# Sample attention of a hybrid decoder layer: the suffix bias added by a small matmul, and cache pages loaded in 32 pieces of 8 KB

## What is computed

```python
kp = cache_k[page_table].reshape(DB, past, H, Dh)      # 8 sequences x 16 pages x 128 tokens
vp = cache_v[page_table].reshape(DB, past, H, Dh)
lfp = cache_logf[page_table].reshape(DB, past, H).astype(jnp.float32)
suffix = (lax.cumsum(lfp, axis=1, reverse=True) - lfp).transpose(0, 2, 1)
cn = jnp.cumsum(logf, axis=1).transpose(0, 2, 1)
s_past = jnp.einsum('bqhd,bkhd->bhqk', q, kp).astype(jnp.float32) * scale
s_past = s_past + suffix[:, :, None, :] + cn[:, :, :, None]
...
p = jax.nn.softmax(jnp.concatenate([s_past, s_new], axis=-1), axis=-1)
o = (jnp.einsum('bhqk,bkhd->bqhd', p[..., :past].astype(v.dtype), vp)
     + jnp.einsum('bhqk,bkhd->bqhd', p[..., past:].astype(v.dtype), v))
```

## Time and profile before

| | before |
|---|---|
| median of 3 runs | 2228.1 us |
| the profiled execution, its own time | 2225.12 us |
| its span, first to last instruction | 2223.5 us |
| sample attention in it | from about 846 to 1119 us |
| mean granted TensorE clock | 0.941 |
| TensorE busy (matmuls) | 1988.0 us, 89% |
| VectorE, ScalarE, GpSimd busy | 591.6, 303.0, 190.3 us |
| DMA | 401.00 MB in 100543 packets, mean 180 GB/s |

### The profile page before, as it was taken

One profiled execution on the slowest core, in us unless ns is written; L12 is line 12 of the kernel. 1 busy time (PEld: TensorE's weight loads), 2 busy tenths in 40 slices (PEclk: granted clock), 3 DMA queues, 4 the chain that ended last, 5 costly groups with the idle time before them and its releaser, 6 DMA issues. The chain is left out here.

```text
span 2223.5 us, 22907 instructions
## 1 busy us (share of the span) xinstructions
PE 1988.0 (89%) x8429; PEld 1087.9 (49%) x8429; DVE 591.6 (27%) x1287; ACT 303.0 (14%) x489; POOL 190.3 (9%) x280
## 2 busy tenths in 40 slices
PE   8999989799999992877689999479999999994997
PEld 4474445466666662545455555334444444441443
DVE  4201124222222222434223222611111111101776
ACT  1000001122222220323211000000000000000111
POOL 1000013000000001123300000000000000001221
PEclk9989999899999995989789999679999999996999
DMA  6020100701020007999742123279999999993220
GB/s 241 14 78 1 41 20 1 290 30 68 30 72 30 31 24 231 263 317 301 244 167 80 48 76 146 85 285 402 419 418 424 425 419 420 422 370 105 69 79 28
DMA packets 100543, 401.00 MB, mean 180 GB/s; under 512 B 18809, under 2 KB 28090, under 8 KB 87634
## 3 DMA queue, kind: packets, MB, share of 16 engines
q1 hardware_dynamic: 76866, 326.02, 38.4%
q0 software_dynamic: 16496, 56.15, 7.5%
q10 hardware_dynamic: 7072, 17.38, 2.0%
HBM read 353.69 MB, written 45.81 MB: 180 GB/s over the span
## 5 line engine op out<-in xcount | busy, mean ns | idle before, releaser
L1791 PE MATMUL psum<-arena 128*64 128x512 f32 (+1 forms) x1024 | 343.8, 598 | 1.4 <-DVE arena L1881 1.4
L774 PE MATMUL psum<-arena 128*128 128x363 f32 (+1 forms) x768 | 256.7, 477 | 13.9 <-DMA arena<-in_w_in 11.2
L1791 PEld LDWEIGHTS psum<-arena 128*64 128x64 f32 (+1 forms) x1024 | 130.0, 165 | 180.9 <-issue 179.1
L287 PE MATMUL psum<-arena 128*128 128x512 f32 x432 | 189.6, 599 | 0.3 <-DMA arena<-in_w_in 0.3
L774 PEld LDWEIGHTS psum<-arena 128*128 128x128 f32 x768 | 139.7, 192 | 84.6 <-DMA arena<-in_w_in 11.3
L1828 PE MATMUL psum<-arena 128*64 128x512 f32 (+1 forms) x512 | 170.0, 595 | 1.0 <-DVE arena L1895 1.0
L975 PE MATMUL psum<-ident,arena 128*128 128x128 f32 x512 | 80.0, 306 | 66.4 <-DMA arena<-in_cache_k 50.1
L287 PEld LDWEIGHTS psum<-arena 128*128 128x128 f32 x432 | 82.3, 193 | 100.7 <-issue 99.9
L1387 PE MATMUL psum<-arena 128*128 128x512 f32 x288 | 125.7, 594 | 1.6 <-PEq L1244 1.6
L2154 PE MATMUL psum<-arena 128*128 128x512 f32 x288 | 125.1, 592 | 0.0
L1828 PEld LDWEIGHTS psum<-arena 128*64 128x64 f32 (+1 forms) x512 | 66.1, 163 | 101.9 <-issue 101.9
(11 more groups left out here) (262 smaller groups left out, 1943.8 us busy)
## 6 DMA issues: line engine op xcount, KB each, us to landing
arena<-in_w_exp_gate SPq DMA_DIRECT2D x32, 2048.0 KB, 13.6
arena<-in_w_exp_up SPq DMA_DIRECT2D x32, 2048.0 KB, 14.1
arena<-in_w_exp_down SPq DMA_DIRECT2D x32, 2048.0 KB, 10.7
arena<-in_cache_v POOLq DMA_DIRECT2D x128, 256.0 KB, 6.6
arena<-in_cache_k SPq DMA_DIRECT2D x128, 256.0 KB, 9.5
arena<-in_w_in SPq DMA_DIRECT2D x9, 2048.0 KB, 10.8
moe_out<-arena ACTq DMA_DIRECT2D x24, 512.0 KB, 11.8
moe_out<-arena SPq DMA_DIRECT2D x1, 9728.0 KB, 38.0
```

Source lines behind the costliest of these rows:

```text
L287: last = mm(c.bank[4 + r % 3][:, :], HT[:, k, t * P:(t + 1) * P], W[:, n + 1, k, :], start=(k == 0), stop=(k == KD - 1))
L774: last = mm(c.bank[7][:, 0:b - a], WG[:, blk % 2, k, q * P:(q + 1) * P], HT[:, k, a:b], start=(k == 0), stop=(k == KD - 1))
L1791: last = mm(out[rows_, :], XT[:, u % 2, k, rows_], c.ring_tile(LOAD[kind, u, r])[:, k, :], start=(k == 0), stop=(k == KD - 1))
```

## The change

The bias is no longer copied to each row by DMA. One load for each sequence brings the 8 heads' rows into 8 partitions (SUF), and a product with an 8 x 128 matrix of zeros and ones (SPREAD, made once by VectorE from the identity) writes head h's bias into the rows of head h of the scores' bank; the four strip products then accumulate onto it. The reduction on VectorE stays, and reads a tile of zeros (NONE) in the bias's place. A page is loaded as 32 pieces: partition g * 32 + q takes tokens 4q to 4q + 3 of page g, which are 8 KB in one run. Keys, bias and values so get another order of tokens, the same for all three: column r * 128 + m is token 4m + r of the chunk. The waits follow: TensorE waits for the bias and the matrix, SP for the scores (`chunk_mm`) in place of the reduction (`ttr`), and no longer for `blanked`.

```diff
@@ -890,7 +890,9 @@
-    NBIAS = view(c, V_AT, 2, PAST)
+    SUF = view(c, V_AT, 2, PAST)[0:H]
+    SPREAD = view(c, HT_AT + 2 * WBLK, P)[0:H]
+    NONE = view(c, HT_AT + 2 * WBLK + P, CH * P)
@@ -927,23 +929,20 @@
             sp.wait_ge(c.sufd_out, 16 * H)
-            sp.wait_ge(blanked, 1)
             for n, w in enumerate((c.w_up_a, c.w_up_b)):
                 sp.dma_start(view(c, UP_AT + n * WBLK, KF, D), w).then_inc(c.up_in, 16)
             for b in range(DB):
                 if b >= 2:
-                    sp.wait_ge(ttr, NCH * (b - 1))
-                for h in range(H):
-                    at = STRIP * (h // 2) + DT * (h % 2)
-                    sp.dma_start(NBIAS[at:at + DT, b % 2, :], c.sufd[h, b:b + 1, :].to_broadcast([DT, PAST])
-                                 ).then_inc(bias_in[b % 2], 16)
+                    sp.wait_ge(chunk_mm, NCH * (b - 1))
+                sp.dma_start(SUF[:, b % 2, :], c.sufd[:, b, :]).then_inc(bias_in[b % 2], 16)
...
-                        sp.dma_start(KC[:, ch, g, :], c.cache_k[bass.ds(page * P, P), :]).then_inc(k_in[ch], 16)
+                        sp.dma_start(KC[g * STRIP:(g + 1) * STRIP, ch], c.cache_k[bass.ds(page * P, P), :].rearrange("(q r) d -> q r d", r=CH)
+                                     ).then_inc(k_in[ch], 16)
@@ -959,7 +958,8 @@
-                        pool.dma_start(VC[:, ch, g, :], c.cache_v[bass.ds(page * P, P), :]).then_inc(v_in[ch], 16)
+                        pool.dma_start(VC[g * STRIP:(g + 1) * STRIP, ch], c.cache_v[bass.ds(page * P, P), :].rearrange("(q r) d -> q r d", r=CH)
+                                     ).then_inc(v_in[ch], 16)
@@ -982,9 +982,15 @@
                 if n >= 2:
                     pe.wait_ge(ttr, n - 1)
+                if n == 0:
+                    pe.wait_ge(blanked, 4)
+                if ch == 0:
+                    pe.wait_ge(bias_in[b % 2], 16 * (b // 2 + 1))
+                mm(c.bank[ch % 2][:, :].rearrange("p (r m) -> p r m", r=CH), SPREAD, SUF[:, b % 2, ch * 512:(ch + 1) * 512].rearrange("h (m r) -> h r m", r=CH),
+                   start=True, stop=False, skip_group_check=True)
                 for j in range(NPAIR):
-                    last = mm(c.bank[ch % 2][strip(j), :], QB[:, b % 2, strip(j)], KTS[:, ch % 2, j, :], start=True,
-                              stop=True)
+                    last = mm(c.bank[ch % 2][strip(j), :], QB[:, b % 2, strip(j)], KTS[:, ch % 2, j, :], start=False,
+                              stop=True, skip_group_check=True)
@@ -1138,12 +1144,10 @@
-                if ch == 0:
-                    dve.wait_ge(bias_in[p], 128 * (b // 2 + 1))
                 dve.wait_ge(chunk_mm, n + 1)
                 v.memset(pace[:, p, ch:ch + 1], 0.0)
                 v.tensor_tensor_reduce(S[:, p, ch * 512:(ch + 1) * 512], c.bank[ch % 2][:, :],
-                                       NBIAS[:, p, ch * 512:(ch + 1) * 512], 1.0, 3e38, ALU.add, ALU.min,
+                                       NONE, 1.0, 3e38, ALU.add, ALU.min,
@@ -1190,7 +1194,13 @@
-            v.memset(NBIAS, 0.0).then_inc(blanked, 1)
+            v.memset(NONE, 0.0).then_inc(blanked, 1)
+            v.memset(SPREAD, 0.0).then_inc(blanked, 1)
+            dve.wait_ge(blanked, 2)
+            cells = SPREAD.rearrange("h (j s) -> h j s", s=STRIP)
+            for half in range(2):
+                v.tensor_copy(cells[:, :, half * DT:(half + 1) * DT], bcast(c.ident[0:H, half:H:2], DT)
+                              ).then_inc(blanked, 1)
```

## The result

The changed kernel takes 2301.4 us (median of 4 runs, 2301.2 to 2303.8) against 2228.0 us (2225.5 to 2229.5) for the kernel before in the same comparison: ratio 1.033, 95% interval 1.0315 to 1.0351. It is 73 us slower. The sign and the cause were as forecast; the forecast size, 45 us, was too small.

A forecast was written before the change was run, and what follows sets the result against it. Prediction: DMA would bound attention, with pages at half rate: 298 us of pages plus 10 of w_up from 852, then 4, end at 1164 against 1119, 45 us later, so 2273 us; range 2212 to 2305.

The forecast's parts named there:

- Pages over 32 partitions: K and V page loads in sample attention: about half rate, 225 GB/s (ends 190 and 300); chance 0.70 together with C.
- The sum: Attention stage: 298 us of pages plus 10 of w_up from 852, last page 1160, stage end 1164, 45 us later.
- rival A: Pages keep full rate: first keys at 878.5, stage end 1103, 16 us earlier, 2212 us; chance 0.20.
- The spread product: TensorE's chain before each chunk's four strips: 0.88 to 1.76 us each, 28 to 56 us in all, hidden behind late pages.
- Bias loads out: 64 bias loads become 8 in attention: some 40 us of DMA time saved, first keys about 5 us earlier.
- GB/s of 200 to 240 at a share near 1: Sign of the main case: DMA rate and share expected all through the attention stage.
- First keys not before 884: Sign of the main case: first keys no earlier than 884 us, since half-rate V pages share the engines with w_up.
- Waits for transfers "well over 70 us": Sign of the main case: TensorE's waits for cache_v and cache_k in sum, with none for VectorE worth naming.
- GpSimd's issue time: Sign of the main case: GpSimd's time to issue stays near 540 ns as before.
- B: Full rate but dear strided product, 1.42 to 1.76 us: 2229 to 2240, TensorE the bound; 0.10 together with overlapping halves.
- C: Page loads do not become 8 KB packets, 2 KB remain: time as forecast, only packet count shows it; within the 0.70.

## Why the prediction was right, and where it fell short

**Pages over 32 partitions: right.** I took 225 GB/s; the pages run at 222 once TensorE leaves them free, and the two ends, 190 and 300, held it. I had 209 for half of the full rate and a little overlap on top; turning the halves in the order of issue adds a further 6% (222 to 236). The reading of a limit at the receiving side held for the pages (every fourth partition: 406 GB/s); that the bursts meet the same limit is left over once their source is ruled out (eight different rows: 189), and is not shown. By the Trainium skill (SBUF — State Buffer, Door 1) partitions 0 to 63 share half of the ports; the runs with 64 partitions (241 GB/s) and with turns (236) agree with that.

**The sum: it stopped at the bytes, and this step failed.** I had the pages flow without a gap from 852 and the last one land at 1160, with 4 us after it. The contiguous product shows the error by itself: it has no dear product and still takes 66 us more than its before, not 45. Its share is 1.02 until 1140 and then 0.62 and 0.82. The last sequence's value pages may not start before the previous weighting has freed their slots, and then GpSimd needs 17.6 us to issue 16 of them; in the changed kernel the stage ends 25.6 us after the first of them (1169.75 to 1195.35). I knew this pace, and used it for the rate and for rival A, but not for the last round of my own sum.

In the changed kernel the transfers end at 1190 (209 GB/s in 1188 to 1190, 12 in the next 2 us), 30 us after my 1160. The missing parts of a share of 1 are 9.8 us from 920 to 960, 1 in 1140 to 1160 and 11.6 from 1160 to 1180; from there to 1190 the share is 0.97. That is 10 for the dip and 13 for the tail. At 222 in place of 225 GB/s the bytes take 4 more. The 3 left over no run explains; they fit the start, where I had w_up alone at 418 GB/s and it moved together with the value pages, at 245: its second half landed 38.5 us after its issue, 21.7 before the change. After 1190 the stage takes 5 us for my 4. So the miss of 31 us on the stage is the tail, 13, the dip, 10, the rate, 4, and some 4 at the two ends. The tail is read from the traces; no run shortened it.

That 2301 lies between my 2240 and 2312 is in part luck: those ends came from the rate alone, 300 and 190 GB/s, the rate was nearly the middle one, and what filled the distance was not in the sum.

**The spread product: named, but too cheap, and not quite hidden.** Contiguous I had 0.88 us and it takes 1.13 (the 0.88 came from products in a long row, see the last section); with the step of four my upper end was 1.76 and it takes 2.05. It also brings the granted clock down and so lengthens its neighbours. TensorE's chain, which "ends near 1115 to 1125 without waits and is hidden", was a sum for the whole stage, and TensorE had less room than I read: it was busy 12.8 to 17.2 of 20 us before, not 13 to 16. By turns, TensorE holds key and value slots too long, the queues run dry (920 to 960), and that time is not made up: 7 to 10 us by the comparison with and without the step, whose trace has no such dip. That is the visible part of this term, for which I had put nothing.

**Bias loads out: right in kind.** The pages with loads against pages with the product are 27 us apart beneath slow pages, where DMA time is what counts. This would fit my 40 us, less what the product takes there, but no run separates the two. At full rate the gain is 12 us and the first keys come 7 us earlier (I said 5).

**The signs.** GB/s of 200 to 240 at a share near 1: seen, with the gaps above. First keys not before 884: 894.9, as the value pages moved slowly beside w_up (245 GB/s in 860 to 880, 289 before). Waits for transfers "well over 70 us": wrong, 61.8, because TensorE was busy with the products in that time; without them it is 100.5. A total of waits shows a transfer bound only if the waiter has nothing new to do. GpSimd's issue time: 492 ns in place of 538, of no consequence.

**The rivals.** A put full rate with a cheap product at 2212; with full rate restored it is 2213.7, so its total was right and its condition was not met. In the total two errors partly cancel: the product took 36 us where I had 28, and the transposes and the weighting with values, at a higher clock, gave back 11.6 us (72.9 against 80.0 and 33.2 against 37.7) where I had 8. B's condition was half met: the product is dear. Its price, 2229 to 2240, was not: 2262, since 2.05 us and the clock were not in it. C: the change does make 8 KB packets (the last sequence's 16 value pages move in 768 packets, 512 of them of 8 KB), and they are worth nothing here. Of the value pages' packets I had a wrong picture: before the change they already were 64 of 4 KB a page, not 128 of 2 KB.

Open: whether the clock falls behind strided products because of the reading itself. No run changed the step without changing the time that TensorE spends in it.

## What to carry to other kernels

Read the DMA share and the GB/s side by side: a full share at half the bytes meant here that the receiving partitions lie together, and a destination stepped over all 128 cures it where a longer piece alone does not. A gather's layout and the product that reads in its order are one decision; keep a float32 moving operand of TensorE within a step of two (37.3 us here, against 65.5 at four), and change one of the two at a time, since beneath a slow transfer a dear product looks almost free. In a sum by bytes, add the last round by itself: when its buffers come free, how fast its transfers can be issued, and what follows.

## What the runs showed of the hardware that I had not expected

- The strided product took the granted clock from 0.95 to 0.84 over 900 to 1100 us, although TensorE was busier (190 against 172 us), and transposes and strips grew with it by 20% and 31%. A step of two left it at 0.96. It fell at the product's end without any idle time of TensorE.
- 64 neighbouring partitions take pages hardly faster than 32, where both turn between the halves: 241 against 236 GB/s.
- A product that stands alone costs more than one in a long row: 1.13 us a pair against 0.88. That it uses 8 of 128 rows is not shown to matter: its shortest instruction takes 587 ns and that of the full-width product 592, and 432 of the latter are busy for 189.6 us only, so in a row they overlap.
- ScalarE's reordering copy of 8 x 512 takes 1.05 to 1.1 us, where its evictions of 128 x 512 take 0.60.
